# A three-stage transformer block on one core: low rank projection in fp32, turned heads between the gate's turns, an eighth ring place, and the last rows written in halves

## What is computed

```python
# layer 1: adaLN modulation, grouped attention, spatial gating, then 16 experts of 32 rows each
aff = softmax(h @ w_router);  gate, idx = top_k(aff.T, 32)
hid = silu(xe @ w1[e]) * (xe @ w3[e]);  y += scatter(gate * (hid @ w2[e]), idx)     # 16 experts
x   = rmsnorm(x1 + gt2 * y, g_final)
# layer 2 ("even"): low rank (MLA) heads and sliding-window heads with sinks
h = rms_norm(x, g_in);  z = h @ w_in                    # cq 256, ckv 128, kpe 32 | q_s 512 | k_s, v_s | gate 1024
q  = rms_norm(cq, g_q_a) @ w_q_up;  kv = rms_norm(ckv, g_kv_a) @ w_kv_up
x  = x + (concat(mla(q, kv, rope(kpe)), swa(q_s, k_s, v_s, sinks)) * silu(gate)) @ w_out
# layer 3 ("odd"): 16 heads with a forget gate
x  = x + (causal(q, k, v, cumsum(log_sigmoid(f))) * silu(gate)) @ w_out
out = rms_norm(x, g_final_2)
```

## Time and profile before

| | us |
|---|---|
| median of 3 runs | 1380.98 |
| lowest, highest | 1378.92, 1387.71 |
| profiled execution, device time | 1373.01 |
| its span (first to last instruction) | 1371.2 |
| PE / DVE / ACT / POOL busy | 979.1 / 403.5 / 240.2 / 89.4 |

### The profile page before, as it was taken

How to read it: one execution, slowest core, us unless ns; L and a number is a source line. 1 busy time by engine, 2 the same in 40 slices (tenths; PEclk the granted TensorE clock), 3 DMA queues, 4 the chain that set the end, 5 groups by cost and what they waited for, 6 DMA issues and landing times.

```text
span 1371.2 us, 15258 instructions
## 1 busy us (share of the span) xinstructions
PE 979.1 (71%) x6623; PEld 499.6 (36%) x6623; DVE 403.5 (29%) x954; ACT 240.2 (18%) x483; POOL 89.4 (7%) x129
## 2 busy tenths in 40 slices
PE   4999997666665665655566655666655697999987
PEld 3765832212211111111111111111111396999876
DVE  4767411011011100101011010101101366885685
ACT  3535110000000000000000000000000354643462
POOL 1200000000020000000000000000000054300030
PEclk9999999879897888888877788787888997999999
DMA  9996989999999999999999999999999651343411
GB/s 398 378 382 246 391 349 428 427 428 428 427 428 428 427 427 428 428 429 428 428 427 427 428 428 428 428 427 428 428 428 427 288 178 50 119 172 137 185 62 47
DMA packets 34771, 482.47 MB, mean 352 GB/s; under 512 B 3854, under 2 KB 3856, under 8 KB 5520
## 3 DMA queue, kind: packets, MB, share of 16 engines
q1 hardware_dynamic: 34240, 479.92, 83.6%
q10 hardware_dynamic: 288, 1.05, 0.2%
q0 software_dynamic: 176, 0.53, 0.1%
HBM read 480.43 MB, written 1.05 MB: 351 GB/s over the span
## 4 chain that ended last, share of the span: by engine, by line
DMA 58%; PE 31%; DVE 7%; ACT 2%; issue 1%; SPq 0%; POOL 0%; POOLq 0%; DVEq 0%
DMA ring<-in_t_w 56%; PE PS L508 7%; PE PS L1023 6%; PE PS L496 4%; PE PS L1069 2%; DMA ring<-in_t_mod 2%; PE PS L485 2%; PE PS L1254 2%; PE PS L697 2%; DVE RR L466 1%; PE PS L793 1%; DVE S L646 1%; PE PS L1011 1%; PE PS L815 1%; DVE S L610 1%
## 5 line engine op out<-in xcount | busy, mean ns | idle before, releaser
L1023 PE MATMUL PS<-ring,S 128*32 128x512 f32 x2016 | 321.2, 771 | 217.7 <-DMA ring<-in_t_w 215.2
L1069 PE MATMUL PS<-ring,S 128*32 128x512 f32 x1008 | 170.0, 809 | 107.6 <-DMA ring<-in_t_w 99.5
L1023 PEld LDWEIGHTS PS<-ring,S 128*32 128x32 f32 x2016 | 63.0, 127 | 455.4 <-DMA ring<-in_t_w 338.2
L514 DVE COPY S<-PS 128x512 f32<-128x512 f32 (+2 forms) x47 | 32.0, 683 | 316.4 <-PE PS L1069 292.0
L508 PE MATMUL PS<-SR,RR 128*128 128x256 f32 x736 | 117.3, 285 | 0.0
L1069 PEld LDWEIGHTS PS<-ring,S 128*32 128x32 f32 x1008 | 33.4, 129 | 226.9 <-DMA ring<-in_t_w 151.7
L508 PEld LDWEIGHTS PS<-SR,RR 128*128 128x128 f32 x736 | 103.8, 189 | 0.7 <-issue 0.6
L454 ACT ACTIVATE RR<-ring 128x1024 fp32r<-128x1024 f32 (+3 forms) x95 | 89.2, 1004 | 38.4 <-DMA ring<-in_t_e_a 18.2
L1602 DVE TENSOR_SCALAR S<-PS,KC 128x256 f32<-128x256 f32 x16 | 7.7, 483 | 279.3 <-PE PS L1053 279.3
L516 ACT ACTIVATE S<-PS 128x512 f32<-128x512 f32 (+2 forms) x50 | 28.0, 570 | 345.2 <-PE PS L485 340.2
L466 DVE TENSOR_TENSOR RR<-ring,RR 128x1024 fp32r<-128x1024 f32 (+2 forms) x76 | 84.1, 1155 | 9.7 <-ACT RR L454 9.7
(11 more groups left out here) (312 smaller groups left out, 997.2 us busy)
## 6 DMA issues: line engine op xcount, KB each, us to landing
ring<-in_t_w SPq DMA_DIRECT2D x189, 2048.0 KB, 31.4
ring<-in_t_mod SPq DMA_DIRECT2D x12, 2048.0 KB, 12.7
ring<-in_t_out SPq DMA_DIRECT2D x6, 2048.0 KB, 7.9
S<-in_t_w SPq DMA_DIRECT2D x3, 2048.0 KB, 13.7
ring<-in_t_e_g SPq DMA_DIRECT2D x2, 2048.0 KB, 7.7
ring<-in_t_o_q SPq DMA_DIRECT2D x2, 2048.0 KB, 7.9
ring<-in_t_o_k SPq DMA_DIRECT2D x2, 2048.0 KB, 8.4
ring<-in_t_o_v SPq DMA_DIRECT2D x2, 2048.0 KB, 8.3
```

Source lines behind the costliest of these rows:

```text
L514: lane.e.tensor_copy(dst, src).then_inc(*lane.mark(out_of(key), *names))
L1023: m = pe.e.matmul(PS[32 * j:32 * j + 32, b, :], expert_rows(2 * k + kk, e_, e_ + 1), place[name, e_, k][:, kk, 512 * j:512 * j + 512], sta ...
L1069: m = pe.e.matmul(PS[q:q + 32, b, :], HT[e_ % 2][:, 128 * s + 32 * j:128 * s + 32 * j + 32], place["w2", e_, j][:, s, 512 * dh:512 * dh + ...
```

## The change

1. **Ring.** `NSLOT` is 8. The first expert piece goes into the new place, which has no earlier owner. The lent places become 8, 9 and 10, the tables get one entry more. After the experts, the fixed pairs give way to a rotation through seven places (`TURNS`). `("e","a")` needs no second place, `("e","kvs")` uses one for both parts. The space comes from a smaller scratch area for DMA descriptors that GpSimd writes; the loads of `positions_2` and `g_final_2` move from POOL's queue to ACT's and SP's.
2. **Low rank projection in fp32.** ACT multiplies the weight by its gain in place, and PE multiplies the state `XT` itself by it in fp32, one matmul instead of three. DVE adds the last expert's rows without a pause, and `ss` stands between the two row tiles.
3. **Turned heads.** PE makes `QMT` after two gate turns and `KMT` after four. The first part of the gate is multiplied in another order: in its first two turns the products that need only the high part of the weight, then the rest. ACT makes the high parts of g1 earlier and those of g0 later; DVE's `x2` moves behind the copies of `QMT`.
4. **Gate's end.** At step 0 of both attentions `gate_finish` comes before the maxima of step 1.
5. **Last rows.** The factor takes two steps on POOL after the last sum. DVE and ACT scale half a row tile each; SP and ACT store half each.

```diff
-NSLOT = 7
+NSLOT = 8
-    FIRST = (3, 4, 2, 7, 8, 5, 6, 0, 1, 9)
-    PAIRS = ((3, 2), (5, 6), (0, 1))
+    SLOTS = (7, 3, 4, 2, 5, 6, 0, 1)
+    FIRST = (7, 3, 4, 2, 8, 9, 5, 6, 0, 1, 10)
+    TURNS = (5, 6, 0, 1, 7, 3, 2)
+    LATER = [(6, None), (0, 1), (7, 7), (3, 2)] + [(TURNS[2 * n % 7], TURNS[(2 * n + 1) % 7]) for n in range(len(later) - 4)]
...
+                lead = half == halves[0] and n2 == 0
...
+                        group = [hi_hi, lo_hi, hi_lo] if not lead else [hi_hi, hi_lo] if q < 2 else [lo_hi]
...
+        def low_rank(i):
+            b = banks.take(("za", i), ALL6)
+            pe.wait_ge(banks.was["za", i])
+            for k in KORD:
+                pe.wait_ge(("weighted", k), ("xa", E - 1, k))
+                m = pe.e.matmul(PS[:, b, 0:416], XT[:, k, 128 * i:128 * i + 128], place["e", "a"][:, k, :], start=k == KORD[0],
+                                stop=k == KORD[-1])
...
-        for _ in range(4):
-            turn(side)
         for src, name in ((QK, "QMT"), (KM, "KMT")):
+            for _ in range(2):
+                turn(side)
             pe.wait_ge("qk" if name == "QMT" else "km")
...
         largest_even(0)
+        turned_heads(QMT, "QMT")
+        dve.wait_ge(*[("sqs", c) for c in range(4)], *[("he", k) for k in range(8)], ("za", 1))
+        for k in range(8):
+            t = dve.e.scalar_tensor_tensor(out=XT[:, k, :], in0=XT[:, k, :], scalar=c_gf[:, k:k + 1], in1=RB[:, 1, :],
+                                           op0=ALU.mult, op1=ALU.mult)
+        t.then_inc(*dve.mark("x2"))
         divide_even(0)
...
             if n:
                 turned_out(dve, "e", n - 1, 1, A2_PT, 2)
+            else:
+                gate_finish(dve, "e", late)
             largest_even(n + 1)
             if n:
                 divide_even(n)
-            gate_finish(dve, "e", late)
+                gate_finish(dve, "e", late)
...
+            if h:
+                act.wait_ge(("rsf", i), ("y4", i, 0))
+                act.settle(act.e.activation(Y4[:, i, 0:512], Y4[:, i, 0:512], ACT.Copy, scale=rsf[:, i:i + 1]), ("result", i, 0))
+                act.e.dma_start(rows_out[:, i, 0:512], Y4[:, i, 0:512]).then_inc(sem_of("s_out"), 16)
```

More of the change, by code:

```diff
@@ L295, in body @@
     later += [(("o", n), 512) for n in ("q0", "q1", "k0", "k1", "v0", "v1", "g0", "g1")] + [(("out3", h), 512) for h in range(2)]
-    for n, (key, w) in enumerate(later):
+    TURNS = (5, 6, 0, 1, 7, 3, 2)
+    LATER = [(6, None), (0, 1), (7, 7), (3, 2)] + [(TURNS[2 * n % 7], TURNS[(2 * n + 1) % 7]) for n in range(len(later) - 4)]
+    for (key, w), (slot, hslot) in zip(later, LATER):
         k_ = 2 if key == ("qup",) else 8
-        unit(key, unit_rows("t_" + "_".join(map(str, key)), k_, w), k_, w, *PAIRS[n % 3])
+        unit(key, unit_rows("t_" + "_".join(map(str, key)), k_, w), k_, w, slot, hslot, hoff=2048 if slot == hslot else 0)
         if key == ("qup",):
-            unit(("kvup",), unit_rows("t_kvup", 1, 1024), 1, 1024, *PAIRS[n % 3], off=1536, hoff=1536, share=key)
+            unit(("kvup",), unit_rows("t_kvup", 1, 1024), 1, 1024, slot, hslot, off=1536, hoff=1536, share=key)
     def used(key):
@@ L690, in gate_matmuls @@
                         pe.wait_ge(banks.was[key])
[L691 removed]
+                    nn = q % 2 if lead else q // 2
                     n = 2 * n2 + nn
[L693 to L698 removed]
+                    for k in range(8) if lead else range(4 * (q % 2), 4 * (q % 2) + 4):
+                        pe.wait_ge(("hi", ukey, k - k % 2) if lead and q < 2 else ("split", ukey, k))
+                        hi_hi, lo_hi, hi_lo = products(ukey, h, k, slice(128 * n, 128 * n + 128), slice(0, 256), swap=True)
+                        group = [hi_hi, lo_hi, hi_lo] if not lead else [hi_hi, hi_lo] if q < 2 else [lo_hi]
+                        for m_, (l_, r_) in enumerate(group):
+                            m = pe.e.matmul(PS[:, b, 256 * nn:256 * nn + 256], l_, r_,
+                                            start=k == 0 and m_ == 0 and (q == 0 or not lead),
+                                            stop=k == 7 and m_ == len(group) - 1 and (q == 3 or not lead))
                     if q == 3:
@@ L773, in sp_program @@
             after(key)
+        sp.wait_ge(*[("o", "done", m_) for m_ in range(4)])
+        sp.e.dma_start(g2b, A["g_final_2"].partition_broadcast(P)).then_inc(*landed("g_final_2"))
+        for i in (1, 0):
+            sp.wait_ge(("result", i, 1))
+            sp.e.dma_start(out.rearrange("(t p) d -> p t d", p=P)[:, i, 512:1024], Y4[:, i, 512:1024]).then_inc(
+                sem_of("s_out"), 16)
     def pe_program(pe):
@@ L1107, in pe_program @@
         for n2 in range(2):
-            straight(pe, ("qst", n2), ("e", "qs"), HE, n2, final=n2 == 1)
+            straight(pe, ("qst", n2), ("e", "qs"), HE, n2, final=n2 == 1, first="he")
             if n2 == 0:
@@ L1730, in dve_program @@
             turn(side)
-        for dst, name in ((QMT, "QMT"), (KMT, "KMT")):
-            for hp in (1, 3):
-                dve.wait_ge((name, hp), "qk", out_of(("kvup", 1, 1)), "km")
-                copy_out(dve, (name, hp), dst[0:96, 2 * hp:2 * hp + 2, :],
-                         PS[0:96, banks.of[name, hp], :].rearrange("p (h t) -> p h t", h=2))
+        turned_heads(KMT, "KMT")
         dve.wait_ge(*[out_of((name, hp)) for name in ("QMT", "KMT") for hp in range(4)])
@@ L1860, in dve_program @@
                 turned_out(dve, "o", n - 1, 1, A3_PT, 2)
+            else:
+                gate_finish(dve, "o", late)
             largest_odd(n + 1)
@@ L1863, in dve_program @@
                 divide_odd(n)
-            gate_finish(dve, "o", late)
+                gate_finish(dve, "o", late)
             turn(side)
@@ L2125, in act_program, with turned_heads @@
                     *act.mark(out_of(("kvup", i, o))))
[L2126 removed]
+        def turned_heads(dst, name):
+            for hp in (0, 2):
+                act.wait_ge((name, hp), "qk", out_of(("kvup", 1, 1)), "km")
+                copy_out(act, (name, hp), dst[0:96, 2 * hp:2 * hp + 2, :],
+                         PS[0:96, banks.of[name, hp], :].rearrange("p (h t) -> p h t", h=2))
         def exponents_even(n):
@@ L2134, in act_program @@
         exponents_even(0)
+        turned_heads(QMT, "QMT")
+        hi_all(act, ("e", "g0"))
         side = gate_act(act, "e", (1, 0), (("out2", 0), ("out2", 1)))
@@ L2137, in act_program @@
             turn(side)
-        for dst, name in ((QMT, "QMT"), (KMT, "KMT")):
-            for hp in (0, 2):
-                act.wait_ge((name, hp), "qk", out_of(("kvup", 1, 1)), "km")
-                copy_out(act, (name, hp), dst[0:96, 2 * hp:2 * hp + 2, :],
-                         PS[0:96, banks.of[name, hp], :].rearrange("p (h t) -> p h t", h=2))
+        turned_heads(KMT, "KMT")
         for n in range(len(A2) + 1):
```

137 lines of the change are left out of this document (59 added, 78 removed).

## The result

| | before | after |
|---|---|---|
| median, us (6 runs each, side by side) | 1378.35 | 1360.74 |
| lowest, highest | 1376.86, 1387.71 | 1357.97, 1369.74 |
| profiled execution, device time | 1373.01 | 1363.62 |
| its span | 1371.2 | 1361.8 |

The ratio is 0.9878 [0.9853, 0.9902]: 1.2% faster, 17.6 us between the medians, where 10.0 were forecast. Yet the two profiled executions are only 9.4 us apart, close to the forecast. Two things bring that about: the profiled execution of before was a quick one, in a stretch that the change rebuilds, as the experiments show, and that of the changed kernel began its experts late.

The account below looks back on a forecast made before the run. DMA was taken to bound the experts (180 to 1079 us), PE's program the rest after 1083. Terms 4.9 + 2.1 + 1.5 + 0.8 + 0.7 = 10.0 us took the median from 1381.0 to 1371.0, range 1361 to 1379.

Parts of the forecast that it names:

- Range and size: Whole kernel: median 1361 to 1379 us, point 1371.0, 0.7% less; under 1% counts as no change, chance 0.65.
- Low rank projection: Scatter to qst: fp32 tiles and ss take 14.8 us against 16.9, 2.1 us less (0.5 to 3).
- The fifth case: Slower: PE stays at 1.2 GHz through the new fp32 projection passes, 4.8 us slower, 1385.8; chance 0.08.
- Ring: Expert weight stream: eighth place takes one piece into idle DMA earlier, 4.9 us less (0 to 5.3).
- Turned heads, gate: Even attention: DVE's chain delays step 1's scores, the gate turn follows at once; 1.5 us less (-1 to 5).
- `x2`: DVE's eight multiplications in the even attention, six slowed beside POOL: 5.0 us, against 3.26 when POOL rests.
- Odd gate's end: Odd attention: PE's 1.15 us wait for gate_finish goes, about 0.4 given back; 0.8 us less (0 to 1.5).
- last rows: Kernel's end: one POOL step fewer, scaling and stores halved; 0.7 us less (0.3 to 1.3).
- POOL's waits: Even attention: PE's waits of 1.76 and 1.48 us for POOL's low parts of g1 go.
- case 4: Eighth place gives nothing, the DMA gap at 174 grows by 4.9 us: sum 5.1, 1375.9; chance 0.08.
- Case 2: DVE clear of POOL, KMT's bank free at 1144: attention gives 5, sum 13.5, 1367.5; chance 0.22.
- third case: Full lock: six x2 each wait for a POOL low part, 1.1 us each; sum 8.7, 1372.3; chance 0.13.

Follow-up runs that it names:

- the second trace: The kernel before, run again with nothing edited, for another trace and more times: median 1379.42 us, ratio 1.0015 to before.
- the fill alone: Kernel before, arithmetic untouched, plus 28 throwaway fp32 matmuls in the four gaps of the first projection tile: 1374.49 us, ratio 0.9974 to before.
- gate_end_back: Changed kernel with gate_finish back behind the first scores' maxima in both attentions: 1363.17 us, ratio 0.9916 to before.
- the third place: Changed kernel with DVE's x2 moved behind the maxima of step 1's scores, where DVE idles: 1352.30 us, ratio 0.9819 to before.
- split_back: Changed kernel with the low rank projection back in three TF32 passes over split halves: 1367.50 us, ratio 0.9916 to before.
- after_filled: Changed kernel plus 12 throwaway 128x128 fp32 matmuls ahead of each of the last expert's w2 pieces: 1361.67 us, ratio 0.9906 to before.
- x2_back: Changed kernel with DVE's eight x2 instructions back behind kst, as in the kernel before: 1361.82 us, ratio 0.9884 to before.

## Why the prediction was right and wrong

- **Range and size: wrong, by one step.** "It lies 8 us below the median of the runs, 1381.0; the gain is the same on both." It isn't. The profiled execution was below the median in good part because it kept the full clock in the old projection, 45.14 us from scatter to scores where the second trace has 51.37. The change removes the stretch that varies: in the changed kernel it takes 44.43 and 44.49. So 6 of the 8 us should have been added to the gain. Of 77 further runs of before, eight were at 1371.3 to 1374.1 us, the rest from 1375.5 to 1387.6; all eight show a mean granted clock of 0.860 or more, of the other 69 only 14 do. So the quick ones may be of the same kind, though only the one trace shows it. The starting point moved as well: the median of 1381.0 was one of three runs, that of six is 1378.35.
- **Luck:** the 9.4 us between the two profiled executions agree with 10.0 by chance. Behind the start of the experts they are 11.6 us apart, and the changed kernel's began them 2.15 us later. Nor do the terms agree one by one: 6.2 for the ring, 0.65 from scatter to scores, 2.8, 1.2 and 0.6 behind them.
- **Low rank projection:** 2.1 forecast (0.5 to 3), 6.7 and 7.1 measured by the medians, 5.7 and 5.0 by the ratios. This is the term that was mis-sized. Its own parts held: 5.83 for 5.75 a tile, 3.63 for 3.3. What it was set against was too short: the old program took 16.9 us to `qst` at the full clock, and the second trace shows that it needn't keep it; that it mostly doesn't is argued from the medians. In the kernel before, the fill alone gives 4.3 of the 7.1. The second new tile lost 1.7 us to a dip. The fifth case asked whether the low clock would catch the new passes; it should have asked which of the two programs has the idle time that invites it. The old tile had 1.10, 1.22, 0.24 and 0.88 us idle between 1085.2 and 1093.4 us in the second trace, the new one none.
- **Ring:** 4.9 forecast. The start of the last piece moved from 903.34 to 898.65 us behind the first expert matmul, 4.7. To the scatter it is 5.7 to 6.2, since the last piece itself took 1.92 us instead of 3.49, and 8.0 in the medians. That is above the forecast's bound of 5.3. The transfer was sized right; what wasn't counted stands behind it. The last piece takes 3.2 to 3.6 us in all five traces with seven places and 1.9 in the ten with eight; from 1079.0 to 1082.6 us the clock was 0.53 in the first, and 1.00 from 1074.7 on in the changed kernel. Eleven pieces were under way before 175, the first at 104.26 (103.5 forecast).
- **Turned heads, gate:** 1.5 forecast for the place, with the 2.1 of the projection given back inside it. The chain was right, to the engine and the wait (8 to 11 us forecast, 9.41 measured, though DVE's copy ended it and not ACT's). From the scores of step 0 to those of step 1 that chain was to take 21.1 us (1126.4 to 1147.5) and took 19.95, where before has 19.27. The 3.3 us of the gate's turn straight behind the scores came as forecast, by the order of `gate_finish` (3.3 us in the trace of gate_end_back); they stood under the turned heads, whose own order gives 0.6 in the medians, which these cannot tell from nothing.
- **`x2`:** 5.0 forecast, 3.71 measured (3.26 before), so it was hardly slowed: POOL was. See below. The next divisions were, as forecast.
- **Odd gate's end** 0.8 forecast, 0.5 measured; **last rows** 0.7 forecast, 0.6 measured; POOL's waits gone, and 6.45 instead of 7.08 at the end.
- **The other cases:** the eighth place gave its piece (case 4 fell), and nothing went slower. Case 2, 1367.5, came nearest by number but not by reason: its condition, an `x2` that isn't slowed, came nearly true, but that is worth 1.3 us (5.0 less 3.71) and not 3.5. The effects measured one by one (8.0, 6.7, 0.6, 3.8) add up to 19.1, against 17.6 together; 1.5 is within what these medians can tell.

## To carry to other kernels

Before a sum is made against a profiled execution that lies below the median of its runs, ask which stretch is quick in it, by a second trace if there is one, and whether the change touches it. Idle gaps in a chain of matmuls can cost more behind them than in them; throwaway work in the gaps is a cheap test. And work that nobody waits for belongs where its engine idles: moving it from one path to another gives nothing, as `x2` showed twice before the third place gave 5.5 us in the traces (8.5 between the medians).

## What the runs showed of the hardware

- **TensorE's clock.** With four gaps in the first projection tile, the level fell to 1.2 GHz at 1093 us for 14 us in one trace of before and not in the other, though both look the same up to there; split_back has it for 20 us. With the gaps filled it stayed at 2.4 GHz in the one trace of each kernel. The Trainium skill ("TensorE: Matmul & The Clock Gate", section "What's actually happening") says that the throttled clock is the default and activity releases it. The fill agrees; that the same program is granted either level, and that the dip in after_filled comes behind 25 us at 1.00 with hardly a pause, shows that idle time before it doesn't settle it alone.
- **DVE and POOL.** In the changed kernel `x2` had begun when POOL's first low part of g0 came, and POOL waited. The timelines of the two over the same microseconds:

```profile
1132.85 2.13 DVE L1744 SCALAR_TENSOR_TENSOR X<-X,KC,cvec 128x256 f32<-128x256 f32 x4
```

```profile
1132.18 2.52 POOL L468 TENSOR_TENSOR RR<-ring,RR 128x256 fp32r<-128x256 f32 x1 [5.43 <-ACT RR L456]
```

  2.52 us for a low part that takes 0.71 on average, while the eight `x2` took 0.46 each. In x2_back POOL was at work first, and they took 0.84 each. The Trainium skill ("SBUF — State Buffer", section "SBUF: two separate sides") calls the shared ports an exclusive lock that goes to whichever instruction starts first, while the other waits. The traces agree that the one that comes later waits. The forecast had taken DVE for the loser; even where it was, in x2_back, 0.84 us each is less than the 1.1 of its third case.
